# NSA attention loop: TensorE takes all scores, all value products and all transposes of a head pair in one visit each

## The reference

```
q, kc, vc, ks, vs, kw, vw, gates = split(h @ w_in)     # 16 heads of 64, 4 key/value groups
o_c = softmax(q k_cmp) v_cmp                           # compressed branch
o_s = softmax(q k_sel, key <= query) v_sel             # 8 selected blocks of 64
o_w = softmax(q kw, key <= query, window 512) vw       # window branch
o = g0 * o_c + g1 * o_s + g2 * o_w
return o @ w_out
```

## Time and profile before

| | |
|---|---|
| median of 3 runs | 2818.9 us (2817.39 to 2819.07) |
| profiled execution, span | 2818.9 us |
| PE busy, weight loads busy | 99%, 83% |
| DVE, ACT, POOL busy | 48%, 35%, 21% |
| the NSA loop, from the first scores | about 820 to 958 us |

### The profile page before, as it was taken

How to read it: one execution, slowest core, us unless ns; L and a number is a source line. 1 busy time by engine, 2 the same in 40 slices (tenths; PEclk the granted TensorE clock), 3 DMA queues, 4 the chain that set the end, 5 groups by cost and what they waited for, 6 DMA issues and landing times. The chain is left out here.

```text
span 2818.9 us, 37840 instructions
## 1 busy us (share of the span) xinstructions
PE 2804.8 (99%) x14520; PEld 2336.6 (83%) x14520; DVE 1342.9 (48%) x1880; ACT 988.0 (35%) x1565; POOL 589.8 (21%) x489
## 2 busy tenths in 40 slices
PE   9999999999999999999999999999999999999999
PEld 7888888888877788888877778888888888888888
DVE  4464543335668654334554455443334365444333
ACT  5332432225166542222432224432224332432222
POOL 0021222203113432220321211222202012222211
PEclk9999999999999999999999999999999999999999
DMA  5323233334520123333322223233333333233331
GB/s 167 90 83 95 78 104 97 95 96 119 150 61 2 39 83 104 90 103 95 111 77 68 82 74 97 72 107 97 94 97 99 100 89 90 72 107 97 95 95 64
DMA packets 460648, 256.09 MB, mean 91 GB/s; under 512 B 9728, under 2 KB 448368, under 8 KB 460400
## 3 DMA queue, kind: packets, MB, share of 16 engines
q1 hardware_dynamic: 459232, 251.69, 30.6%
q10 hardware_dynamic: 1296, 2.75, 0.3%
HBM read 248.11 MB, written 2.10 MB: 89 GB/s over the span
## 5 line engine op out<-in xcount | busy, mean ns | idle before, releaser
L1712 DVE SCALAR_TENSOR_TENSOR w_lo<-w_raw,w_hi 128x1024 fp32r<-128x1024 f32 x461 | 629.5, 1367 | 855.3 <-ACT w_hi L1281 854.6
L572 PE MATMUL acc<-a_hi,w_hi 128*128 128x512 f32 (+1 forms) x2256 | 885.4, 392 | 0.3 <-DVE g_lo L2135 0.3
L574 PE MATMUL acc<-a_hi,w_lo 128*128 128x512 f32 (+1 forms) x2256 | 875.9, 388 | 0.0
L573 PE MATMUL acc<-a_lo,w_hi 128*128 128x512 f32 x2064 | 803.5, 389 | 0.0
L1281 ACT ACTIVATE w_hi<-w_raw 128x1024 fp32r<-128x1024 f32 x460 | 482.8, 1051 | 494.4 <-PE acc L574 481.9
L572 PEld LDWEIGHTS acc<-a_hi,w_hi 128*128 128x128 f32 x2256 | 423.8, 188 | 90.3 <-issue 4.4
L574 PEld LDWEIGHTS acc<-a_hi,w_lo 128*128 128x128 f32 x2256 | 423.5, 188 | 87.9
L573 PEld LDWEIGHTS acc<-a_lo,w_hi 128*128 128x128 f32 x2064 | 387.7, 188 | 79.6 <-issue 1.9
L574 PE MATMUL acc<-hid_hi,w_lo 128*128 128x512 f32 (+1 forms) x704 | 264.5, 376 | 0.0
L573 PE MATMUL acc<-hid_lo,w_hi 128*128 128x512 f32 (+1 forms) x704 | 264.5, 376 | 0.0
L572 PE MATMUL acc<-hid_hi,w_hi 128*128 128x512 f32 (+1 forms) x704 | 264.5, 376 | 0.0
(11 more groups left out here) (353 smaller groups left out, 3450.4 us busy)
## 6 DMA issues: line engine op xcount, KB each, us to landing
w_raw<-ffn_w_gate SPq DMA_DIRECT2D x88, 512.0 KB, 3.8
w_raw<-ffn_w_up SPq DMA_DIRECT2D x88, 512.0 KB, 3.8
w_raw<-gm_w_in SPq DMA_DIRECT2D x64, 512.0 KB, 4.1
w_raw<-ffn_w_down SPq DMA_DIRECT2D x64, 512.0 KB, 3.7
w_raw<-ret_w_in SPq DMA_DIRECT2D x48, 512.0 KB, 3.8
w_raw<-gm_w_out SPq DMA_DIRECT2D x32, 512.0 KB, 3.8
w_raw<-ffn_w_down SPq DMA_DIRECT2D x32, 384.0 KB, 3.4
w_raw<-nsa_w_in SPq DMA_DIRECT2D x21, 512.0 KB, 4.2
```

The costliest lines, as they stand in the source:

```text
L572: pe.matmul(o_bank, lhs_hi, rhs_hi, start=start, stop=False)
L573: pe.matmul(o_bank, lhs_hi, rhs_lo, start=False, stop=False)
L574: return pe.matmul(o_bank, lhs_lo, rhs_hi, start=False, stop=stop)
L1712: dve.scalar_tensor_tensor(w_lo[:, slot, :, :], w_raw[:, slot, :, :], 1.0, w_hi[:, slot, :, :].bitcast(f32), ALU.mult, ALU.subtract).then_ ...
```

## The change

The steps are reordered: chunk 1 first, then chunks 2 and 0, then chunk 3. For each pair TensorE scores all three steps, then multiplies the values of the pair before, then transposes all three steps, then the factors of this pair. DVE's order becomes: probabilities of the last step of `g-1`, the maxima of the three steps of `g`, the inverse sums of `g` (before: of `g-1`), the scaled output of `g-1`, the probabilities of steps 0 and 1. ACT copies the factors of `g` (before: of `g-1`) after the exponentials of `g`. GpSimd makes the factors of `g` before it adds the output of `g-1`, and splits after the addition. At the end the first projection pieces lie between the last value products, in another order. The TensorE and DVE part, and the others:

```diff
-PARTS = [[(3, 0)], [(1, 0)], [(2, 0), (0, 3 * P)]]
-WIDTH = [4, 2, 4]
+PARTS = [[(1, 0)], [(2, 0), (0, 3 * P)], [(3, 0)]]
+WIDTH = [2, 4, 4]
 STEPS = [(br, hp, kind) for br in range(2) for hp in range(H_NSA // 2) for kind in range(len(PARTS))]
-
-SCORED = [tuple(s + k for k in kinds) for s in range(0, len(STEPS), len(PARTS)) for kinds in ((0, 1), (2,))]
...
-                for m in range(len(SCORED) + 2):
-                    for s in SCORED[m] if m < len(SCORED) else ():
...
+                def score(s):
+
+                    br, hp, kind = STEPS[s]
+                    bank = step_bank(s)
+
+                    wait(pe, pt_done, s - 2)
...
+                def turn(v):
+
+                    for x in range(2):
+                        pe.wait_ge(exp_done, exps_through(v - 1) + (x + 1) * len(PARTS[STEPS[v][2]]))
+                        for k in range(WIDTH[STEPS[v][2]]):
+                            last = pe.transpose(step_bank(v)[:, x, k * P:(k + 1) * P], step_rows(v)[:, x, k * P:(k + 1) * P], ident[:, :])
+                    last.then_inc(t_mm, 1)
+
+                def weigh(v):
+
+                    br, hp, kind = STEPS[v]
+                    pe.wait_ge(pt_done, v + 1)
...
+                    last.then_inc(pv_mm, 1)
+
+                def spread(g):
+
+                    pe.wait_ge(rs_inv, g + 1)
+                    wait(pe, spread_done, g)
+                    for c in range(CH):
+                        last = pe.transpose(acc[:, 3, c * P:(c + 1) * P], SS[:, c * P:(c + 1) * P], ident[:, :])
+                    last.then_inc(spread_mm, 1)
+
+                for g in range(H_NSA):
+                    steps = range(len(PARTS) * g, len(PARTS) * (g + 1))
+                    for s in steps:
+                        score(s)
                         if s == 0:
                             cmp_turn(CH - 1)
                         if s == 1:
                             cmp_values(CH - 1)
...
+                    if g:
+                        for s in steps:
+                            weigh(s - len(PARTS))
+                    for s in steps:
+                        turn(s)
+                    spread(g)
+                pe.wait_ge(pt_done, n - 2)
+                out_pieces(0)
+                weigh(n - 3)
+                weigh(n - 2)
+                out_pieces(1)
+                weigh(n - 1)
                 for t in range(2, DT):
                     out_pieces(t)
...
                         if kind == len(PARTS) - 1:
                             if br and hp >= 2:
                                 split_out(hp - 2)
-                            if g:
-                                spread_out(g - 1)
+                            spread_out(g)
                     split_out(H_NSA // 2 - 2)
-                    spread_out(H_NSA - 1)
                     split_out(H_NSA // 2 - 1)
...
                 for g in range(H_NSA + 1):
                     s = len(PARTS) * g
+                    if g:
+                        probabilities(s - 1)
                     if g < H_NSA:
                         maxima(s)
+                        maxima(s + 1)
+                        maxima(s + 2)
+                        inverse_sums(g)
                     if g:
-                        probabilities(s - 1)
-                        inverse_sums(g - 1)
+                        scaled_out(g - 1)
                     if g < H_NSA:
-                        maxima(s + 1)
-                    if g < H_NSA:
-                        maxima(s + 2)
                         probabilities(s)
                         probabilities(s + 1)
-                    if g:
-                        scaled_out(g - 1)
...
+                    for g in range(H_NSA):
+                        factor(g)
+                        if g:
+                            add_out(g - 1)
+                        if g >= H_NSA // 2 + 2:
+                            output_low(g - H_NSA // 2 - 2)
+                    output_low(H_NSA // 2 - 2)
+                    add_out(H_NSA - 1)
                     output_low(H_NSA // 2 - 1)
```

More of the change, by code:

```diff
@@ L1080, in out_pieces @@
                         piece(L["n_out"], L["o_out"], 1, j, t, o_hi, o_lo)
-                assert len(STEPS) % 3 == 0
                 n = len(STEPS)
-                for m in range(len(SCORED) + 2):
-                    for s in SCORED[m] if m < len(SCORED) else ():
[L1086 to L1101, removed]
-                            for x in range(2):
[L1103 to L1106, removed]
@@ new lines, in score @@
+                def score(s):
+                    br, hp, kind = STEPS[s]
+                    bank = step_bank(s)
+                    wait(pe, pt_done, s - 2)
+                    if s == 0:
+                        pe.wait_ge(kd_dup, 2)
+                        pe.wait_ge(sm_done, CH)
+                    if s == 1:
+                        pe.wait_ge(ocmp_done, CH - 1)
+                    if s == 2:
+                        pe.wait_ge(nv_done, len(VALUES) + 2)
+                        pe.wait_ge(pc_t, CH)
+                    if br and s == n // 2:
+                        pe.wait_ge(n_rope, 12)
+                        pe.wait_ge(kd_dup, 4)
+                    for c, col in PARTS[kind]:
+                        for x in range(2):
+                            last = pe.matmul(bank[:, x, col:col + (c + 1) * P], nq[side_of(x), hp, c * P:(c + 1) * P],
+                                             kd[side_of(x), br, hp // 2, 0:(c + 1) * P], start=True, stop=True)
+                            if c == PARTS[kind][-1][0]:
+                                last.then_inc([s_even, s_odd][x], 1)
@@ new lines, in turn @@
+                def turn(v):
+                    for x in range(2):
+                        pe.wait_ge(exp_done, exps_through(v - 1) + (x + 1) * len(PARTS[STEPS[v][2]]))
[5 more added lines that the diff above has]
+                    pe.wait_ge(pt_done, v + 1)
+                    if v == 0:
+                        pe.wait_ge(ocmp_done, CH)
+                    if kind == 0:
+                        wait(pe, o_rd, v // len(PARTS))
+                    for c, col in PARTS[kind]:
+                        for kb in range(c + 1):
+                            for x in range(2):
+                                last = pe.matmul(acc[side_of(x), 0, c * P:(c + 1) * P], vt[:, br, kb, hp // 2 * HD:(hp // 2 + 1) * HD],
+                                                 pt[:, 2 * (v % 3) + x, col + kb * P:col + (kb + 1) * P], start=kb == 0, stop=kb == c)
+                    last.then_inc(pv_mm, 1)
@@ L1110, in attention @@
                             cmp_values(CH - 1)
[L1111 to L1143, removed]
@@ L2086, in scaled_out @@
                     dve.tensor_tensor(work[:, g % 2, :], acc[:, 0, :], work[:, 2, :], ALU.mult).then_inc(o_rd, 1)
-                last_part = len(PARTS) - 1
                 for g in range(H_NSA + 1):
                     s = len(PARTS) * g
+                    if g:
+                        probabilities(s - 1)
                     if g < H_NSA:
                         maxima(s)
+                        maxima(s + 1)
+                        maxima(s + 2)
+                        inverse_sums(g)
                     if g:
-                        probabilities(s - 1)
-                        inverse_sums(g - 1)
+                        scaled_out(g - 1)
                     if g < H_NSA:
-                        maxima(s + 1)
-                    if g < H_NSA:
-                        maxima(s + 2)
                         probabilities(s)
                         probabilities(s + 1)
-                    if g:
-                        scaled_out(g - 1)
             dve.memset(ones[:, :], 1.0).then_inc(ones_ready, 1)
@@ L2378, in output_low, with factor @@
                         pool.tensor_tensor(o_lo[:, hp, :], o_sum_t[:, hp, :], o_hi[:, hp, :].bitcast(f32), ALU.subtract).then_inc(o_lo_done, 1)
-                    for g in range(H_NSA):
+                    def factor(g):
                         br, hp = divmod(g, H_NSA // 2)
@@ L2388, in _, with add_out @@
                                            gates.unsqueeze(3).broadcast_to(over), ALU.mult).then_inc(rs_inv, 1)
[L2389 to L2392, removed]
+                    def add_out(g):
                         pool.wait_ge(ocmp_done, CH)
@@ L2396, in _ @@
                             pool.wait_ge(o_add, g)
+                        hp = g % (H_NSA // 2)
                         pool.tensor_tensor(o_sum_t[:, hp, :], o_sum_t[:, hp, :], work[:, g % 2, :], ALU.add).then_inc(o_add, 1)
+                    for g in range(H_NSA):
[6 more added lines that the diff above has]
+                    add_out(H_NSA - 1)
                     output_low(H_NSA // 2 - 1)
```

## The result

| | before | after |
|---|---|---|
| median | 2818.8 us (2817.39 to 2819.44, 6 runs) | 2828.3 us (2827.46 to 2829.11, 6 runs) |
| ratio, 95% interval | | 1.0035 (1.0025 to 1.0045) |
| span of the profiled execution | 2818.9 us | 2827.4 us |
| head pair: first branch, second branch | 7.96, 8.23 us | 8.62, 8.62 us |

The change costs 9.5 us; forecast were 2830.3 us and +11.4.

A forecast was written before the change was run, and what follows sets the result against it. DVE and PE were both nearly full, DVE with 7.02 us of work in 7.96. Start 2.7, loop 9.6 and end -0.9 sum to +11.4 on 2818.9: 2830.3 us, range 2826.3 to 2837.

The forecast's parts named there:

- likeliest case: The forecast itself, 77%: DVE idles 1.73 us a pair before the inverse, waiting for ACT's sums; period 8.76, 2830.3 us.
- M0: DVE's maxima of a pair's first part, 256 wide; 0.64 us forecast, its start being 0 of the period.
- M1, M2: DVE's maxima of the 384+128 part and the 512-wide part; forecast to start at 0.64 and 2.02, through at 3.35.
- P0, P1, P2: DVE's copies of the three parts' probabilities; forecast 0.62, 1.14 and 1.14 us, the last just before the next M0.
- S0, S1: PE's scores of the next pair's 256-wide and 384+128 parts; forecast at 7.0 and 7.8, slack 0.8 and 0.3.
- Rival A: In the loop: the inverse's wait is hidden and both DVE idle terms go, -14.7 us there, 2805 us; 5%.
- the lead: Time from the start of M0 to ACT's first exponential of that pair, forecast 0.47 us.
- Rival B: In the loop: the inverse's wait is hidden in part, period 8.35, 2824.6 us, no change by measure; 6%.
- Rival C: GpSimd's factors delay PE's factors and next first scores beyond 0.8 us slack; 7.5 us more, 2838 us; 8%.
- Rival D: PE's clock falls to half in T, making PE's work set the period; +102 us, some 2932 us; 4%.
- T: PE's visit for all transposes of a pair, then its factors; twelve transposes and the factors forecast at 1.89 us.
- T2: PE's transposes of the third part, forecast to wait for ACT's last exponential and end near 5.6, needed at 7.62.

The follow-up runs named there:

- inv_mid: Changed kernel with DVE's inverse moved between P0 and P1, the scaled output of the pair before going ahead of P0: 2818.5 us, 1.0001.
- prev_sums: Changed kernel, same DVE order, but the inverse waits for and reads the row sums of the pair before (output wrongly scaled): 2810.7 us, 0.9972.
- act_more: Changed kernel plus one unused 128x512 copy on ACT in each pair, ahead of the last exponentials: 2837.1 us, 1.0065.
- t0_before_values: inv_mid_s0_first plus PE's first transposes ahead of the value products and DVE's P0 ahead of the scaled output: 2818.6 us, 0.9997.
- inv_mid_s0_first: inv_mid plus PE taking the factors of a pair behind the next pair's first scores: 2816.5 us, 0.9992 against the kernel before.
- pool_more: Changed kernel plus one unused 128x512 multiply on GpSimd ahead of each pair's factor: 2834.7 us, 1.0052.
- split_last: Kernel before, with ACT's copy of the factors ahead of its split of an output tile: 2817.4 us, 0.9993.
- parts_old: Changed kernel's new visits with the old part order (chunk 3, chunk 1, chunks 2 and 0): 2832.7 us, 1.0052.
- s0_first_2: The code of inv_mid_s0_first, unchanged, timed again: 2816.4 us, 0.9992 against the kernel before.

## Why the prediction was right

The likeliest case came true, mechanism and place; the time is 2.0 us under the forecast and inside the range. The period, with 0 at the start of M0:

| step | predicted | measured |
|---|---|---|
| first exponential after M0 | 0.47 | 0.54 |
| ACT's exponentials | 4.51 | 4.46 |
| M1, M2, maxima done | 0.64, 2.02, 3.35 | 0.68, 2.06, 3.36 |
| last sum to inverse | 0.10 | 0.04 |
| inverse starts; DVE's idle time | 5.08; 1.73 | 5.04; 1.68 |
| inverse, scaled output | 0.11, 0.67 | 0.12, 0.60 |
| P0, P1, P2 | 0.62, 1.14, 1.14 | 0.59, 1.13, 1.14 |
| factors on PE, S0, S1 | 6.5, 7.0, 7.8 | 6.42, 7.00, 7.62 |
| period | 8.76 | 8.62 |

- **The inverse's wait.** The three runs that touch it alone settle it: moved, it gives the loss back (inv_mid); its cause taken away, 1.15 us a pair go (prev_sums); 0.52 us more on ACT cost 0.52 (act_more). Rival A, hidden, would have needed ACT's chain under 2.9 us; it is 4.46.
- **The size.** 0.14 us a pair were too much. Half of it is the scaled output: its 0.67 in the earlier trace rows was a distance to the maxima, 878.51 to 879.18, and here, with a copy behind it, it is 0.60. The rest is the step after ACT's sums (0.10 taken, 0.04 found), ACT's exponentials (0.05), the copy P0 (0.03), and the lead, 0.07 the other way. Rival B at 8.35 was further off than the forecast.
- **From the first M0 of the loop to the last value products** the change was to add 11.4 us; it adds 11.0: the 134.20 us from 822.66 to 956.86 became 145.23, from 819.98 to 965.21. Part of that nearness is luck: 1.6 of the 11.0 are a fall of the clock that the prediction didn't have, and about as much was put too high in the loop. Without the fall the stretch adds 9.4, close to the 9.5 between the medians.
- **The start** grew by 4.1 us, 12.89 from M0 to M0 against 8.76, where 2.7 were forecast. The difference is a fall of the clock that I had not foreseen (last section). Its price shows in two kernels that do the same up to there: 12.29 from M0 to M0 in t0_before_values, with the fall, and 10.70 in inv_mid_s0_first, without, so 1.6; without it, 2.5 here.
- **The loop**: 120.89 us for 14 pairs against 113.01, so +7.9 for 9.6; it is the 0.14, times 14, less 0.2 by which the second pair was longer than the others (8.85).
- **The end**: 11.45 against 12.43 us, -1.0 for -0.9.
- **Around the span.** "Nothing is added" was wrong, and harmless by luck: in all runs whose span is listed the device time is 1.7 to 1.8 us more (2829.11 for 2827.4). The profiled execution of before with its 2818.9 was thus itself 1.8 us above the median; the first 34 us of it took 2.7 us longer than in that of after, from where both run alike up to the loop. That is why the spans differ by 8.5 and the stretch by 11.0.
- **Rival C**: not in the change, and shown by pool_more to begin 0.72 us away. **Rival D**, the clock falling in T: not borne out. 20 transposes of exponentials, the 4 of the factors and PE's wait for GpSimd filled 3.47 us at a granted clock of 1.00 in the pair shown. The rule of the Trainium skill, "TensorE: Matmul & The Clock Gate", section "Part 4: PE-mode transpose", that transposes don't count as busy for the clock as matmuls do, is not seen at work in T, and no window of 10 us between 830 and 960 us is under 1.00; for T the measurement decides. The fall at the loop's start came behind idle time and four transposes, and no run tells whether the transposes had a part in it.
- **One sign didn't show, and it cost nothing.** PE's weight loads were to wait for ACT in T. In the pair shown they don't: PE reaches T2 at 4.90 (881.08), when its first head's exponentials are through, and its second head after the last of them, which ends at 5.00. T2 is done at 5.94, where 5.6 was forecast, and P2 comes at 7.48. The weight loads do wait for GpSimd, as forecast.
- **Where the visits' gain is.** The change removes 0.77 + 0.17 of DVE's waits and 0.08 of its work, and adds 1.68: +0.66, which is 8.62 - 7.96. In the second branch it is +0.39, since the split of the output tile, 0.27 us a pair before (split_last), is hidden now, as forecast.

What stays open: whether inv_mid_s0_first is faster than the kernel before. Its loop is (7.81 a pair for 7.96 and 8.23), but its first pair takes 1.9 us more (10.70 from M0 to M0 for 8.76), and an advantage of 1.7 us is just what these intervals can't tell from none. Why its first pair is longer was not tried.

## What to carry to other kernels

An engine that takes its work in order should not meet, right behind the work that feeds another engine's chain, an instruction that needs the chain's end: put the independent work between them (here one line, worth 10 us). To price such a wait, lay the other engine's instructions end to end from the first input it gets, and compare with when the waiting engine arrives; its busy share (here 59%) says nothing. Fewer and larger visits remove bubbles (0.16 us a pair for one visit in t0_before_values), but they also push the last input of each group to its end, so ask for each group who waits for its last element.

## What the runs showed of the hardware

**TensorE's clock fell at the loop's start, for 3.4 us.** In the kernel after PE waited 2.04 us for DVE, did four transposes and eight score products, and then the granted clock was at half, the lower of its two levels, 1.2 GHz, while PE worked. Its timeline and the window:

```profile
820.12 0.66 PE L1013 MATMUL tr<-ident,ex 128*128 128x128 f32 x4 [2.04 <-DVE ex L2017]
...
821.84 3.57 PE L1022 MATMUL acc<-pc,vblk 128*128 128x128 f32 x16
```

```profile
821.83:825.21 3.38, 3.38 (x18) 3.38 (x16) 1.47 (x8) 0.55 (x3) 0.00 (x0) 0.52 0.02 5
```

The same 16 products took 2.05 us in the kernel before, behind 1.61 us of idle time, and its window is at 1.00:

```profile
822.80 0.66 PE L1015 MATMUL tr<-ident,ex 128*128 128x128 f32 x4 [1.61 <-DVE ex L2005]
...
824.14 2.05 PE L1024 MATMUL acc<-pc,vblk 128*128 128x128 f32 x16
```

```profile
824.14:826.12 1.98, 1.98 (x16) 1.86 (x16) 0.78 (x4) 1.35 (x4) 0.00 (x0) 1.00 0.04 8
```

It isn't the length of the idle time alone: of nine traces with those 2.04 us seven show the fall (16 products in 2.76 to 3.57 us) and the two of inv_mid_s0_first's code don't (2.05), while t0_before_values, in which PE does the same up to there, does (3.51); of three with 1.61 us two show it (split_last 3.50, parts_old 3.33). And in s0_first_2 the clock fell elsewhere, with PE busy without a break:

```profile
784.00:786.00 2.00, 2.00 (x31) 1.96 (x30) 1.27 (x3) 1.95 (x4) 1.00 (x1) 0.94 1.20 290
786.00:788.00 2.00, 2.00 (x6) 1.57 (x6) 1.67 (x3) 1.93 (x4) 0.27 (x1) 0.50 1.19 290
```

That was right behind 16 products of 64 columns and 32 of 31 columns, in four transposes; inv_mid_s0_first ran the same instructions there at 1.00. At the loop's start a fall costs 1.6 us (from M0 to M2 the new part order takes 6.67 to 6.70 us in the seven traces with it, 5.08 and 5.09 in the two without), and the execution of s0_first_2 with the other one took 0.9 more than the fastest. Whether it comes differs between executions of one code, so part of the spread of about 1.5 us within each kernel's times is likely this: of the 22 timed runs of inv_mid_s0_first and s0_first_2, the nine at 2815.5 to 2815.7 us have a mean granted clock of 1.000, the others, at 2816.4 to 2817.1, one of 0.999. What picks it was not tried. A comparison of single executions can't tell 1.5 us in this kernel.

**Small prices.** From ACT's last row sum to DVE's reciprocal 0.04 us; GpSimd's multiply of 128x512 1.00 from start to start, its addition 1.27 to 1.28 in duration; ACT's 128x512 exponential with its row sum 0.71 from start to start (0.61 to its sum's read and 0.10 for that), a plain copy of that size 0.52.
